# Stick-breaking attention: logits of two heads on the two halves of TensorE's rows, the causal mask moved to the scan and the weights, the mixer loops written out

## The reference, cut to what matters

```python
for blk in range(seq // SB_BLOCK):                     # blocks of 128 queries
    start, end = blk * SB_BLOCK, (blk + 1) * SB_BLOCK
    logits = jnp.einsum('bhtd,bhsd->bhts', qh[:, :, start:end], kh[:, :, :end])
    causal = jnp.arange(end)[None, :] < (start + jnp.arange(SB_BLOCK))[:, None]
    log_remain = jnp.where(causal, jax.nn.log_sigmoid(-logits), 0.0)
    log_after = lax.cumsum(log_remain, axis=3, reverse=True) - log_remain
    weights = jnp.where(causal, jnp.exp(jax.nn.log_sigmoid(logits) + log_after), 0.0)
    outs.append(jnp.einsum('bhts,bhsd->bhtd', weights, vh[:, :, :end]))
```

## Time and profile before

| | |
|---|---|
| median of three runs | 1687.5 us (1686.31 to 1690.17) |
| the profiled execution | 1688.82 us, of which 1687.1 us are the span of its instructions |
| PE busy | 1446.6 us, 86% of the span |
| DVE, ACT, POOL busy | 510.7, 361.8, 261.9 us |
| mixers, from their first logits (472.37 us) to their last copy of OB (ends at 757.64 us) | 285.3 us |

### The profile page before, as it was taken

The page is one execution under the profiler, slowest core; times in us unless marked ns, Lnnn a source line. Parts: engine busy times, 40 slices in busy tenths (PEclk is TensorE's granted clock), DMA queues, the critical chain, the costliest instruction groups (busy, mean ns, idle before and its releaser), DMA issues. The chain is left out here.

```text
span 1687.1 us, 17290 instructions
## 1 busy us (share of the span) xinstructions
PE 1446.6 (86%) x6018; PEld 772.1 (46%) x6018; DVE 510.7 (30%) x695; ACT 361.8 (21%) x655; POOL 261.9 (16%) x379
## 2 busy tenths in 40 slices
PE   6999999789989999999994577778787878739997
PEld 4456844434467777774553322223232322214443
DVE  3332033325047666662223211111111111121332
ACT  2221131000044555551221000100010001022221
POOL 1000000100034344432110211111111111100110
PEclk9999999789999999999997698989998989879999
DMA  4221046522331211106110499999999999951220
GB/s 179 75 75 51 1 160 168 146 63 80 75 133 43 65 38 44 37 1 271 52 51 29 175 384 408 390 392 411 393 408 403 403 404 401 394 225 41 81 81 37
DMA packets 107334, 306.45 MB, mean 182 GB/s; under 512 B 22416, under 2 KB 60960, under 8 KB 81440
## 3 DMA queue, kind: packets, MB, share of 16 engines
q1 hardware_dynamic: 97792, 289.16, 45.6%
q0 software_dynamic: 9504, 16.80, 2.6%
HBM read 283.85 MB, written 39.90 MB: 192 GB/s over the span
## 5 line engine op out<-in xcount | busy, mean ns | idle before, releaser
L1532 PE MATMUL pe_gu<-w_gu,xT 128*64 128x512 f32 x1024 | 273.5, 695 | 109.1 <-DMA w_gu<-in_w_expert_up 105.7
L251 PE MATMUL ps<-wide,gst 128*128 128x512 f32 x640 | 284.7, 605 | 2.7 <-DVE wide L404 2.7
L1532 PEld LDWEIGHTS pe_gu<-w_gu,xT 128*64 128x64 f32 x1024 | 83.2, 159 | 277.7 <-issue 275.9
L251 PEld LDWEIGHTS ps<-wide,gst 128*128 128x128 f32 x640 | 123.4, 195 | 153.9 <-issue 152.1
L832 DVE TENSOR_TENSOR_SCAN Pm<-rem,Pm 128x128 f32<-128x128 f32 (+3 forms) x96 | 108.0, 1125 | 76.4 <-ACT brk L766 76.3
L1625 DVE TENSOR_TENSOR hs<-sg,pe_gu 128x256 f32<-128x256 f32 x32 | 13.5, 421 | 382.3 <-ACT sg L1596 382.3
L1193 PE MATMUL p_x<-wide,mT 128*128 128x512 f32 x256 | 114.8, 602 | 2.1 <-DVE mx L1125 1.4
L1550 PE MATMUL pe_y<-w_d,hTe 128*64 128x512 f32 x512 | 115.4, 592 | 1.1 <-DVE ys L1630 1.1
L1853 PE MATMUL f_pg<-w_gu,f_xT 128*128 128x512 f32 x256 | 115.2, 604 | 1.1 <-ACT f_xT L1771 1.1
L928 POOL TENSOR_TENSOR wt<-brk,Pm 128x128 f32<-128x128 f32 (+3 forms) x96 | 88.7, 923 | 164.5 <-DVE Pm L832 164.5
L265 PE MATMUL psk<-w_tok,wide 128*128 128x260 f32 (+1 forms) x384 | 111.7, 453 | 0.0
(11 more groups left out here) (281 smaller groups left out, 1490.5 us busy)
## 6 DMA issues: line engine op xcount, KB each, us to landing
w_gu<-in_w_expert_gate SPq DMA_DIRECT2D x64, 1024.0 KB, 14.0
w_gu<-in_w_expert_up SPq DMA_DIRECT2D x64, 1024.0 KB, 16.1
w_d<-in_w_expert_down SPq DMA_DIRECT2D x64, 1024.0 KB, 9.3
gst<-in_w_in SPq DMA_DIRECT2D x20, 512.0 KB, 4.3
y_sb<-y_d SPq DMA_DIRECT2D x8, 1024.0 KB, 5.3
qkv_d<-y_sb SPq DMA_DIRECT2D x12, 512.0 KB, 2.6
qk_st<-rows_d SPq DMA_DIRECT2D x8, 768.0 KB, 7.1
gst<-qkv_d SPq DMA_DIRECT2D x8, 768.0 KB, 5.4
```

Of the source, the lines that this page charges most:

```text
L251: last = pe.matmul(ps[s][:, c], w_ct[:, s, k, :], hT[:, k, c], start=k == 0, stop=k == KT - 1)
L1532: last = pe.matmul(p_gu[e * CAP:(e + 1) * CAP, :], xT[:, s, k, e * CAP:(e + 1) * CAP], wv[:, e, :, k, :], start=k == 0, stop=k == KT - 1)
```

## The change

- Two heads go together. The 8 iterations become 4 pairs of heads by 2 rounds (`ROUNDS`): round A has query blocks 0, 2, 6, 7 of both heads, round B blocks 1, 3, 4, 5. Strips of the two heads (`e` = 0, 1) alternate, again 12 to a round (4864 keys in A, 4352 in B).
- The queries and keys of head `e` lie in partitions `64 e` to `64 e + 63`. PE issues the logits of both heads one after the other, every second step, into LB[0] and LB[1].
- The -1e30 matmul is gone. In a strip with the diagonal (8 of 12) the scan takes a second operand `past` (1 from the diagonal on, 0 elsewhere) with max, and POOL sets the masked part of wt to 0 with an affine_select of 128x128 after its product, behind a semaphore of its own (`w_step`).
- The steps go on through the rounds without the three extra ones at the end. The pieces are spread over 24 positions: 0, 2, 5, 8, 10, 13, 16, 18, 21.
- OB is copied at step 3 of the next round, in two copies (`attended`).
- LT is gone: PE reads decay_kk itself. The four products by col_q on DVE (L887) become one of 128x512.
- The loops are written out, and waits count from the start of the stage.
- The queries and keys are loaded once per pair (1024 KB, 4 times) and not once per head (512 KB, 8 times).

```diff
-STRIPS = [(t, c0, min(c0 + 512, (t + 1) * P)) for t in range(NT) for c0 in ((512, 0) if t >= 4 else (0,))]
-NS = len(STRIPS)
+ROUNDS = ((0, 2, 6, 7), (1, 3, 4, 5))
+STRIPS = [[(t, n, c0, min(c0 + 512, (t + 1) * P), e) for n, t in enumerate(ts) for c0 in ((512, 0) if t >= 4 else (0,)) for e in range(2)]
+          for ts in ROUNDS]
+NS = len(STRIPS[0])
...
-            return [p for n, p in enumerate(pieces) if n * (2 * STEPS) // len(pieces) == pos]
+            return [p for n, p in enumerate(pieces) if n * 2 * NS // len(pieces) == pos]
...
+                def logits(g):
+                    t, n, c0, c1, e = at(g)
...
+                    if e == 0:
+                        reach(pe, sig_done, g)
+                    d = slice(e * SD, (e + 1) * SD)
+                    pe.matmul(LB[e][:, 0:c1 - c0], qk_st[d, g2 % 2, 0, t * P:(t + 1) * P], qk_st[d, g2 % 2, 1, c0:c1],
+                              start=True, stop=True).then_inc(log_done, 1)
...
+                for g in range(G + 3):
+                    if g < G and g % 2 == 0:
+                        logits(g)
+                        logits(g + 1)
+                    if g < G:
+                        for p in pieces_at(2 * (g % NS)):
+                            delta(p, g // NS)
+                    if 2 <= g < G + 2:
+                        transposes(g - 2)
+                    if g >= 3:
+                        weighted(g - 3)
+                    if g < G:
+                        for p in pieces_at(2 * (g % NS) + 1):
+                            delta(p, g // NS)
...
+                for g in range(G + 2):
+                    if g < G:
+                        breaks(g)
+                        for p in pieces_at(2 * (g % NS)):
+                            delta(p, g // NS)
+                    if g >= 2:
+                        evacuate(g - 2)
+                    if g >= NS and g % NS == 3:
+                        attended(g // NS - 1)
...
+                    dve.wait_ge(sig_done, g + 1)
+                    if first:
+                        reach(dve, w_done, g - 1)
+                    else:
+                        dve.wait_ge(scan_done, g - 1)
+                    held = past[:, 512 - m:] if first else rem[:, e, 0:m]
+                    dve.tensor_tensor_scan(Pm[:, e, o + c0:o + c1][:, ::-1], rem[:, e, 0:m][:, ::-1], held[:, ::-1],
+                                           Pm[:, e, o + c1:o + c1 + 1], ALU.mult, ALU.max if first else ALU.bypass).then_inc(scan_done, 1)
...
+                    pool.tensor_tensor(wt[:, g % 3, 0:m], brk[:, e, 0:m], Pm[:, e, o + c0 + 1:o + c1 + 1], ALU.mult).then_inc(
+                        w_step if first else w_done, 1)
+                    if first:
+                        pool.wait_ge(w_step, sum(at(f)[3] == (at(f)[0] + 1) * P for f in range(g + 1)))
+
+                        pool.affine_select(out=wt[:, g % 3, m - P:m], in_=wt[:, g % 3, m - P:m], compare_op=ALU.is_gt, fill=0.0, base=0,
+                                           pattern=[[-1, P]], channel_multiplier=1).then_inc(w_done, 1)
```

More of the change, by code:

```diff
@@ L593, in pieces_at, with reach @@
         def pieces_at(pos):
-            return [p for n, p in enumerate(pieces) if n * (2 * STEPS) // len(pieces) == pos]
[L597 to L600, removed]
+            return [p for n, p in enumerate(pieces) if n * 2 * NS // len(pieces) == pos]
+        def reach(e, s, n):
+            if n > 0:
+                e.wait_ge(s, n)
         with nc.Block() as block:
@@ L621, in _ @@
                 sp.dma_start(ln_row[:], A["ln_moe"][0:1, :].to_broadcast([P, D])).then_inc(small_in, 16)
[L622 to L630, removed]
+                for i in range(NT - 2):
+                    sp.wait_ge(S_ok, i + 1)
+                    sp.dma_start(gst[:, i % 2], qkv_v[:, :, (i + 2) * P:(i + 3) * P]).then_inc(chunk_in[i % 2], 16)
+                    if i % 2 and i // 2 + 2 < NT // 2:
+                        sp.wait_ge(log_done, (i + 1) * NS)
+                        sp.dma_start(qk_st[:, i // 2 % 2], sqk_v[:, :, i // 2 + 2, :]).then_inc(head_in[i // 2 % 2], 16)
+                    sp.wait_ge(nm_ok, i + 1)
+                    load_z(i + 2)
@@ L632, in _ @@
             @block.tensor
             def _(pe):
[L634 to L646, removed]
@@ L652, in transposes, with weighted @@
+                def transposes(g):
+                    t, n, c0, c1, e = at(g)
+                    pe.wait_ge(w_done, g + 1)
+                    reach(pe, ev_done, g - 1)
                     for b in range((c1 - c0) // P):
-                        last = pe.transpose(TB[k % 2][:, b * P:(b + 1) * P], wt[:, k % 3, b * P:(b + 1) * P], ident[:])
+                        last = pe.transpose(TB[e][:, b * P:(b + 1) * P], wt[:, g % 3, b * P:(b + 1) * P], ident[:])
                     last.then_inc(tr_done, 1)
[L656 to L665, removed]
+                def weighted(g):
+                    t, n, c0, c1, e = at(g)
+                    if g % NS == 0:
+                        reach(pe, at_done, g // NS)
+                    pe.wait_ge(ev_done, g + 1)
+                    m = (c1 - c0) // P
+                    h = g // (2 * NS) * 2 + e
+                    for b in range(m):
+                        last = pe.matmul(OB[:, n, e * SD:(e + 1) * SD], wT[:, e, b * P:(b + 1) * P], v_sb[:, c0 // P + b, h * SD:(h + 1) * SD],
+                                         start=g % NS == 0 and b == 0, stop=g % NS == NS - 1 and b == m - 1)
@@ L780, in delta @@
                     if piece in ("xq", "y2"):
-                        act.wait_ge(xt_done, i * LV + (2 if piece == "xq" else 3))
+                        act.wait_ge(xt_done, i * LV + (1 if piece == "xq" else 2))
                         act.activation(flat(XT), flat(GC), ACT.Copy).then_inc(XT_ok, 1)
-                    if piece == "xq" and not first:
-                        act.wait_ge(O_ok, i + 1)
-                        act.wait_ge(nss_ok, i)
-                        act.activation(nsq[:], mx[:, ds(i - 1, 1), 0:GW].rearrange("p a n -> p (a n)"), ACT.Square).then_inc(nsq_ok, 1)
+                    if piece == "xq" and i > 0:
+                        act.wait_ge(O_ok, i)
+                        reach(act, nss_ok, i - 1)
+                        act.activation(nsq[:], mx[:, i - 1, 0:GW], ACT.Square).then_inc(nsq_ok, 1)
                     elif piece == "vn":
@@ new lines, in scale_w_o, with delta @@
+                def scale_w_o(k):
+                    dve.wait_ge(wo_in, 16)
+                    dve.wait_ge(nw_in, 48)
+                    last = dve.tensor_scalar(w_o[:, k, :], w_o[:, k, :], nw[:, k // GH:k // GH + 1], None, ALU.mult)
+                    if k == KT - 1:
+                        last.then_inc(wo_ok, 1)
+                def delta(piece, i):
+                    s = i % 2
+                    hs = slice(i * GH, (i + 1) * GH)
+                    b3 = lambda x: x.unsqueeze(2).to_broadcast([P, GH, P])
+                    if i == 1 and pieces.index(piece) < KT:
+                        scale_w_o(pieces.index(piece))
@@ L888, in delta @@
+                        dve.tensor_tensor(o.rearrange("p (h n) -> p h n", h=GH), GB[:], b3(col_q[:, hs]), ALU.mult).then_inc(o_step, 1)
                         dve.wait_ge(o_done, i + 1)
-                        dve.wait_ge(o_step, (i + 1) * GH)
-                        o = mx[:, ds(i, 1), 0:GW].rearrange("p a n -> p (a n)")
+                        dve.wait_ge(o_step, i + 1)
                         dve.tensor_tensor(o, o, GC[:].rearrange("p h n -> p (h n)"), ALU.add).then_inc(O_ok, 1)
-                def body(j, s, i, first=False, scale=False):
-                    for k in range(STEPS):
-                        if k < NS:
-                            if STRIPS[k][1] != 0 or STRIPS[k][0] < 4:
-                                dve.wait_ge(w_done, i * NS + max(k - 1, 0) + 1)
-                            scan(i, k)
-                        for p in pieces_at(2 * k) + pieces_at(2 * k + 1):
-                            delta(p, j, s, i, first, scale)
@@ L901, in _ @@
-                body(0, 0, 0, first=True)
-                body(0, 1, 1, scale=True)
-                with dve.Fori(0, NT // 2 - 1) as j:
-                    body(j + 1, 0, 2 * j + 2)
-                    body(j + 1, 1, 2 * j + 3)
+                for g in range(G):
+                    scan(g)
+                    for p in pieces_at(2 * (g % NS)) + pieces_at(2 * (g % NS) + 1):
+                        delta(p, g // NS)
             @block.gpsimd
             def _(pool):
-                pool.sem_inc(w_done, 2)
@@ new lines, in _ @@
+                begin(0)
+                for g in range(G):
+                    i, k = g // NS, g % NS
+                    if k == NS - 2 and i < NT - 1:
+                        begin(i + 1)
+                    if k == 5 and i > 0:
+                        pool.wait_ge(nss_ok, i)
+                        pool.tensor_scalar(nss[:], nss[:], 1.0 / GD, EPS, ALU.mult, ALU.add).then_inc(nms_ok, 1)
```

(3 more changed lines are left out.)

258 lines of the change are left out of this document (100 added, 158 removed).

## The result

The changed kernel takes 1697.26 us (median of 4 runs, 1695.01 to 1700.06) against 1686.9 us for the kernel before beside it: a ratio of 1.0057, 95% interval 1.0039 to 1.0075. It is slower, 0.6% or 10 us, where 1673.5 us was forecast, and 4 us above the upper end of the range.

The account below looks back on a forecast made before the run. PE's own work was taken to bound the mixers: 5.8 us spared less 4.2 us waited, 1.6 us per round, 12.8 in eight plus 1.3, 14 us in all, gave 1673.5 us, with 8 in 10 between 1648 and 1693 us.

Parts of the forecast that it names:

- PE's work: Mixers: shared changeovers spare 1.9 us and half the logits streaming 3.9 us, 5.8 us per round, 46 us in eight.
- third slot: Rival, logits of two heads: passes in strict order overlap only in part, three slots for two; 1684 us, chance 0.14.
- Three waits per round: PE waits at y2 for kd 1.3, vn for R 1.6, weighted(0) for OB's copy 1.3 us: 4.2 per round.
- the way to R: From logits(8, 9) through scan, Sg and R to PE's vn: 5.9 us in A, 4.6 us in B.
- The port, and the price of the select: Scans and POOL's reading operations exclude each other; select 0.3 us. Rival: port becomes the bound, 1696 us at 0.83, chance 0.10.
- The clock: Rival: granted clock falls behind A's waits near 2 us; up to 12 us back, 1686 us; 0.09 with other causes.
- the sum of 14 us: Whole kernel: 5.8 us spared less 4.2 waited per round, 12.8 in eight, plus 1.3 for the round without OB wait.
- Loops, mask matmul: Mixers: written-out loops win nothing, and the mask matmul as such is worth nothing, as the array changes over there anyway.
- the first rival: Mixers: waits shorter than thought; none to two thirds of them gone up to all, 28 to 47 us faster; chance 0.17.

Follow-up runs that it names:

- experiment 5: Logits issued one strip per step, so no two heads stream at once: 1721.17 us on the changed kernel, 1715.31 us on the kernel of experiment 1.
- experiment 1: Changed kernel with vt_kt at position 7 for 8 and ks at 15 for 16: 1659.45 us, ratio 0.984.
- experiment 2: Changed kernel with six idle fp32 matmuls ahead of y2's and of vn's wait for DVE in each round: 1682.1 us, ratio 0.9971.
- experiment 3: Kernel of experiment 1 with two superfluous DVE products ahead of R in every second round, PE's instructions the same: 1681.96 us, ratio 0.9974.
- experiment 6: Kernel of experiment 1 with the mask back on PE and no select: 1658.13 us, ratio 0.9837.
- experiment 8: Kernel before with the mixers' loops written out and nothing else: 1685.5 us, ratio 0.9993.
- experiment 4: Changed kernel with the mask back on PE (two bf16 matmuls per diagonal pair), plain scan, no select: 1693.03 us, ratio 1.0025.

## Why the prediction was wrong, step by step

*PE's work, 5.8 us per round, 46 in all.* Right within what can be told. The mixers grew by 12.7 us; PE's waits in them grew by 35.4 us, from 3.3 to 38.7, and the clock loss by 24: that leaves -47 us, and experiment 5 gives 42 us from the other side. Both heads stream at once (1.06 us for 1.05), where a third slot would have added 0.43 us per pair. The Trainium skill ("TensorE: Matmul & The Clock Gate", Part 3, the mechanism) states that matmuls start in program order. For passes issued one head after the other that would have meant the third slot; the trace has the four starts in pairs, at 600.25 and 600.78, and does not show in which order the passes were issued.

*Three waits per round, 4.2 us.* Right in place and cause, and nearly in size: 36.1 us in all, where the sum had 32.3 (8 x 4.2 less 1.3). Part of that is luck, as single terms were off both ways: in A 1.8 (y2), 1.5 (vn) and 0.9 us (OB) where I had 2.1, 1.9 and 1.3; in B 1.2, 2.25 and 1.0 where I had 0.5, 1.4 and 1.3. In B the way to R was too short in the sum, 4.6 us, and is 5.5 us. From the logits at 603.70 on, the changed kernel's trace has:

```profile
605.08 0.38 ACT L751 ACTIVATE rem<-LB 128x256 f32<-128x256 f32 x1 [1.23 <-POOL wt L902]
...
605.99 0.72 DVE L823 TENSOR_TENSOR_SCAN Pm<-rem,Pm,past 128x256 f32<-128x256 f32 x1
606.14 1.45 POOL L902 TENSOR_TENSOR wt<-brk,Pm 128x512 f32<-128x512 f32 x1 [1.16 <-DVE Pm L823]
...
606.63 1.51 DVE L866 TENSOR_TENSOR Sg<-St,col_last 128x512 f32<-128x512 f32 x1
...
608.07 1.11 DVE L869 SCALAR_TENSOR_TENSOR Rr<-GA,coef,vb 128x128 f32<-128x128 f32 x4
```

The scan begins 2.29 us after the logits, where 1.45 and 0.6 of the port had been taken, as ACT waits for POOL to be done with an older strip. The greater part is Sg: R begins 1.44 us after it, where 0.58 had been taken, since Sg begins within a product of POOL. Experiments 1, 2 and 3 move these waits and the time moves with them.

*The port, and the price of the select.* The median select takes 0.292 us, as taken. The sum of 64 is 30.2 us, as some take longer: one took 1.29 us beside a scan of DVE that ran at the same time. It does not bound the kernel (experiments 1 and 6).

*The clock.* This step failed: the sum of 14 us has no term for it, and it cost 24 us. I had it as a rival, "up to 8 x 1.5 = 12 us would come back: no change", at 0.09 together with others. The size of the stretch was wrong: I took it from the earlier trace rows, where the lower level holds for less than 3.4 us, and here each lasts 10.2 us and costs 4.8. And it comes after B's wait of 2.25 us, which I had put at 1.4 us and not looked at. A's waits of 1.8 and 1.5 us are not followed by one, nor is that of 2.54 us in the first round. In the round with w_out's scaling DVE's ways are longer still, and it comes twice (2.25 us ahead of y2, 2.40 us ahead of vn), at 0.50 both times. With 24 us of clock loss more than before, -14 us becomes +10 us. Experiment 2 fills the waits with work and takes the stretch out behind three of the five stops: the clock loss falls from 26.8 to 8.5 us. Experiment 3 puts the stretches back, with PE's instructions unchanged, and there the waits and the clock loss together make up the difference.

*Loops, mask matmul.* Worth nothing, as said (experiments 8 and 6).

*Slips in the sums of the prediction.* None changes the forecast of the time. With 29.0 us of PE's work and 1 us more in A, its own waits give 35.3 us for an A round and 31.2 for a B round, not 34.5 and 31.5. In the first rival, 28 us faster is reached with about 0.4 of the waits gone; with two thirds gone it is some 36. And a round becomes longer than now from 0.7 us per select on, not 0.65, if LT's 0.7 us are taken off.

What is open: which stops of PE bring the lower level, and for how long. A stop of 2.54 us in the changed kernel did not, nor did those of 1.83 us, but one of 1.64 us with one head at a time did; and experiment 4 has shorter stretches after waits as long. So the length of a stop alone does not tell its price.

## What to carry to other kernels

When PE gets less work between fixed links to other engines, work out each link anew, and move the pieces so that the other engine's part stands ahead of its long operation: here two list positions were worth 38 us, where the whole change with them is 27 us faster than the kernel before. Price a stop of PE by the granted clock of the rows behind it and not by its length alone. If a wait can't be removed, idle matmuls in it can pay.

## What the runs showed of the hardware

Two fp32 matmuls on the two 64-row halves, 512 columns each, take the time of one (1.06 and 1.05 us). A stop of PE of 2.25 us was followed by 10.2 us at a granted clock of 0.50, with PE busy throughout, while one of 2.54 us in the same execution was not. Superfluous matmuls in the place of the stop kept the clock at 1.00 and saved 4.8 us. A DVE operation with two operands in the on-chip memory, Sg, took 1.51 us when it began 0.5 us into one of POOL's products, and 0.66 alone.
